# Attention masks added to the head biases on GpSimd instead of by products into the score banks, in a two-layer hybrid encoder

## The reference

```python
_, sel = lax.top_k(score, n_sel)                      # 64 admissible keys per query
logits = jnp.einsum('bqhd,bqkhd->bqkh', qb, k_sel) * ATTN_SCALE
logits = logits + bias_tab[t5_bucket(sel - qpos[None, :, None])]
logits = jnp.where(valid[..., None], logits, -1e30)
p = jax.nn.softmax(logits, axis=2)
return jnp.einsum('bqkh,bqkhd->bqhd', p, v_sel)
...
_, states = lax.associative_scan(combine, (a_seq, bu), axis=1)   # state-space branch
```

## Time and profile before

| what | us |
|---|---|
| median of 3 runs (1130.84 to 1132.05) | 1131.94 |
| the profiled execution | 1129.84 |
| its span | 1127.7 |
| PE busy in the span | 1115.2 (99%) |
| DVE, ACT, POOL busy | 756.5, 556.5, 405.6 |
| granted PE clock, mean | 0.998 |

### The profile page before, as it was taken

How to read it: one execution, slowest core, us unless ns; L and a number is a source line. 1 busy time by engine, 2 the same in 40 slices (tenths; PEclk the granted TensorE clock), 3 DMA queues, 4 the chain that set the end, 5 groups by cost and what they waited for, 6 DMA issues and landing times.

```text
span 1127.7 us, 17816 instructions
## 1 busy us (share of the span) xinstructions
PE 1115.2 (99%) x6020; PEld 922.6 (82%) x6020; DVE 756.5 (67%) x1082; ACT 556.5 (49%) x795; POOL 405.6 (36%) x567
## 2 busy tenths in 40 slices
PE   9999999999999999999999999999999999999997
PEld 7888778898788888888888888889877888888885
DVE  5656745789877865674586465468897787555544
ACT  6545433574673554454245444436747635454440
POOL 2889986107700478997700000011275000000001
PEclk9999999999999999999999999999999999999999
DMA  8866653645556586565367566536535566757541
GB/s 270 256 205 185 219 183 109 199 136 161 163 179 223 151 238 192 188 222 192 115 187 226 184 227 201 188 99 225 162 115 155 192 202 207 220 165 246 186 149 38
DMA packets 158720, 207.51 MB, mean 184 GB/s; under 512 B 13144, under 2 KB 107672, under 8 KB 158656
## 3 DMA queue, kind: packets, MB, share of 16 engines
q1 hardware_dynamic: 154928, 201.70, 55.9%
q10 hardware_dynamic: 2704, 3.36, 1.1%
q0 software_dynamic: 1024, 1.61, 0.8%
HBM read 205.56 MB, written 1.06 MB: 183 GB/s over the span
## 4 chain that ended last, share of the span: by engine, by line
PE 63%; POOL 18%; DVE 10%; issue 4%; DMA 2%; ACT 2%; SPq 1%; POOLq 0%; DVEq 0%; ACTq 0%
PE ps L719 19%; PE ps L721 18%; PE ps L720 18%; POOL small L1565 7%; DVE wlo L1215 5%; POOL b_bar L1565 3%; POOL tab_c L1565 2%; POOL tab_s L1701 2%; POOL tab_s L1565 1%; POOL tab_c L1698 1%; DVE score L1376 1%; DMA raw<-in_ffn_w_up 1%; PE ps L746 1%; PE ps L952 1%; DMA raw<-in_w_in 1%
## 5 line engine op out<-in xcount | busy, mean ns | idle before, releaser
L1215 DVE TENSOR_TENSOR wlo<-raw,whi 128x1024 fp32r<-128x1024 f32 (+1 forms) x372 | 479.7, 1306 | 197.1 <-ACT whi L411 183.4
L411 ACT CAST whi<-raw 128x1024 fp32r<-128x1024 f32 (+1 forms) x372 | 385.4, 1044 | 289.0 <-PE ps L721 221.1
L719 PE MATMUL ps<-whi,xh 128*128 128x512 f32 x990 | 390.7, 395 | 0.7 <-DVE wlo L1215 0.3
L721 PE MATMUL ps<-whi,xl 128*128 128x512 f32 x990 | 383.3, 387 | 0.0
L720 PE MATMUL ps<-wlo,xh 128*128 128x512 f32 x990 | 383.0, 387 | 0.0
L719 PEld LDWEIGHTS ps<-whi,xh 128*128 128x128 f32 x990 | 185.9, 188 | 43.3 <-issue 5.6
L721 PEld LDWEIGHTS ps<-whi,xl 128*128 128x128 f32 x990 | 185.9, 188 | 38.5
L720 PEld LDWEIGHTS ps<-wlo,xh 128*128 128x128 f32 x990 | 186.1, 188 | 35.3
L1589 POOL TENSOR_TENSOR rstd<-var_eps,cst 128x1 f32<-128x1 f32 x12 | 18.2, 1516 | 528.6 <-DVE var_eps L1262 528.6
L719 PE MATMUL ps<-whi,hh 128*128 128x512 f32 x352 | 139.6, 397 | 0.0
L721 PE MATMUL ps<-whi,hl 128*128 128x512 f32 x352 | 137.3, 390 | 0.0
(11 more groups left out here) (194 smaller groups left out, 1217.0 us busy)
## 6 DMA issues: line engine op xcount, KB each, us to landing
raw<-in_ffn_w_up SPq DMA_DIRECT2D x352, 256.0 KB, 4.0
raw<-in_ffn_w_down SPq DMA_DIRECT2D x176, 256.0 KB, 3.0
raw<-in_w_in SPq DMA_DIRECT2D x128, 256.0 KB, 3.3
raw<-in_w_branch SPq DMA_DIRECT2D x32, 256.0 KB, 3.3
raw<-in_w_out SPq DMA_DIRECT2D x32, 256.0 KB, 3.6
bias_g<-bias_rows ACTq DMA_DIRECT2D x16, 192.0 KB, 4.0
raw<-in_w_in SPq DMA_DIRECT2D x16, 148.0 KB, 2.2
affine<-in_ln_g SPq DMA_DIRECT2D x4, 512.0 KB, 5.3
```

Source lines behind the costliest of these rows:

```text
L411: nc.scalar.copy(whi[:, s % RING, 0:w], raw[:, s % RAW, 0:w]).then_inc(S["hi_done"], 1)
L719: nc.tensor.matmul(o, ah, bh, start=start, stop=False)
L721: return nc.tensor.matmul(o, al, bh, start=False, stop=stop)
L1215: nc.vector.tensor_tensor(wlo[:, s % RING, 0:w], raw[:, s % RAW, 0:w], f32(whi[:, s % RING, 0:w]), ALU.subtract).then_inc(S["split_done"], 1)
```

## The change

The two mask products, `ident_bf` and PE's wait for the mask go. POOL adds the mask to each head's bias window in SBUF (`add_bias`, two instructions a head, 16 a layer), and DVE's logits read the sum, `biased`, in place of `bias_g`. The windows get four buffers instead of two; ACT loads those of heads 0, 1 and of heads 4 to 7 (128 KB each instead of 192 KB), each pair of heads a pair of `exp_probs` earlier than before, and POOL's own queue loads those of heads 2 and 3 once the mask is done, as their buffer lies over the indexer's scores. In slots 7, 11 and 15 the scores now stand ahead of the turn.

```diff
     bias_g = place("bias_g", [P, 2, SEQ])
+    biased = place("biased", [P, 4, 3 * P])
...
+    bias_s = place("bias_s", [P, 2, SEQ])
...
             def load_bias(l, hd):
-                if hd >= 2:
-                    act.wait_ge(S["neg_max_ready"], N_HEADS * l + hd - 1)
+                if hd >= 4:
+                    act.wait_ge(S["bias_ready"], N_HEADS * l + hd - 3)
...
-                if p + 1 < N_PAIRS:
-                    load_bias(l, 2 * p + 2)
-                    load_bias(l, 2 * p + 3)
+                if p + 2 < N_PAIRS:
+                    load_bias(l, 2 * p + 4)
+                    load_bias(l, 2 * p + 5)
...
             def att_scores(l, p):
-                for e in range(2):
-                    nc.tensor.matmul(ps[:, score_bank(e), 0:3 * P], ident_bf[:, :], mask[:, :], start=True,
-                                     stop=False)
...
             def attention(l, j):
+                p, last = divmod(j - SCORES_AT, 4)
+                if last == 0 and 0 <= p < N_PAIRS:
+                    att_scores(l, p)
                 p, last = divmod(j - TRANSPOSE_AT, 4)
                 if last == 0 and 0 <= p < N_PAIRS:
                     prob_transpose(l, p)
-                p, last = divmod(j - SCORES_AT, 4)
-                if last == 0 and 0 <= p < N_PAIRS:
-                    att_scores(l, p)
...
             def att_logits(l, p):
-                    dve.wait_ge(g_landed[e], 16 * (N_PAIRS * l + p + 1))
+                    dve.wait_ge(S["bias_ready"], N_HEADS * l + 2 * p + e + 1)
...
-                            in1=bias_g[:, e, end - KEYS[i]:end][:, ::-1], scale=-1.0, scalar=3.0e38, op0=ALU.add,
+                            in1=biased[:, (2 * p + e) % 4, cols], scale=-1.0, scalar=3.0e38, op0=ALU.add,
...
+            def add_bias(l, p):
+                for hd in (2 * p, 2 * p + 1):
...
+                    if p >= 2:
+                        pool.wait_ge(S["neg_max_ready"], N_HEADS * l + hd - 3)
+                    for i in range(NT):
+                        cols = slice(i * P, i * P + KEYS[i])
+                        ins = nc.gpsimd.tensor_tensor(biased[:, hd % 4, cols], bias_of(hd)[:, 0:KEYS[i]][:, ::-1],
+                                                      mask[:, cols], ALU.add)
+                    ins.then_inc(S["bias_ready"], 1)
...
             def states(l):
-                for q in range(NQ):
-                    rotate_back(l, q)
-                    if q + 2 < NQ:
-                        make_decay(l, q + 2)
+                rotate_back(l, 0)
+                make_decay(l, 2)
+                rotate_back(l, 1)
+                pool.wait_ge(S["mask_ready"], NT * (l + 1))
+                pool.wait_ge(S["bias_stored"], 16)
+                for hd in (2, 3):
+                    pool.dma_start(bias_of(hd), bias_window(hd)).then_inc(early_landed[hd % 2], 16)
+                add_bias(l, 0)
+                add_bias(l, 1)
+                make_decay(l, 3)
+                rotate_back(l, 2)
+                add_bias(l, 2)
+                add_bias(l, 3)
+                rotate_back(l, 3)
```

More of the change, by code:

```diff
@@ L123, in build @@
     ident = sb("ident", [P, P])
-    ident_bf = sb("ident_bf", [P, P], BF16)
     parity = sb("parity", [P, P])
@@ L190, in build @@
     stg_at = at[0]
-    bias_g = place("bias_g", [P, 2, 3 * P])
+    bias_g = place("bias_g", [P, 2, SEQ])
+    biased = place("biased", [P, 4, 3 * P])
     at[0] = stg_at
@@ L195, in build @@
     stg = place("stg", [P, 2, NT, 512])
+    score_at = at[0]
+    bias_s = place("bias_s", [P, 2, SEQ])
+    at[0] = score_at
     score = place("score", [P, NT, SEQ])
@@ L215, in build @@
     x_landed = [sem(f"x_landed{i}") for i in range(3)]
-    g_landed = [sem(f"g_landed{i}") for i in range(2)]
+    g_landed = [sem(f"g_landed{i}") for i in range(4)]
+    early_landed = [sem(f"early_landed{i}") for i in range(2)]
     S = {}
@@ L223, in build @@
                  "proj_done proj_read pt_done pt_read bu_done bu_read decay_ready scan_done states_ready y_used "
-                 "idx_done relu_done weighted idx_added mask_ready s_done neg_max_ready exp_done prt_done prt_read "
+                 "idx_done relu_done weighted idx_added mask_ready bias_ready s_done neg_max_ready exp_done prt_done prt_read "
                  "pv_done inv_ready prob_ready yah_done ya_split bra_read y_sum gelu_done yh_done y_split gm_done "
@@ L304, in score_bank, with bias_of, bias_window @@
         return 4 if hd % 2 == 0 else 2
+    def bias_of(hd):
+        return (bias_g, bias_s)[hd // 2 % 2][:, hd % 2, :]
+    def bias_window(hd):
+        return bass.AP(bias_rows.tensor, hd * 512 + 1 + P, [[1, P], [1, SEQ]])
     def quarter(tab, q):
@@ L562, in load_bias @@
             def load_bias(l, hd):
-                src = bass.AP(bias_rows.tensor, hd * 512 + 1, [[1, P], [1, 3 * P]])
-                if hd >= 2:
-                    act.wait_ge(S["neg_max_ready"], N_HEADS * l + hd - 1)
+                if hd >= 4:
+                    act.wait_ge(S["bias_ready"], N_HEADS * l + hd - 3)
                 else:
@@ L569, in load_bias @@
                     act.wait_ge(S["bias_stored"], 16)
-                act.dma_start(bias_g[:, hd % 2, :], src).then_inc(g_landed[hd % 2], 16)
+                act.dma_start(bias_of(hd), bias_window(hd)).then_inc(g_landed[hd % 4], 16)
             def exp_probs(l, p):
@@ L993, in att_scores @@
                     pe.wait_ge(S["proj_read"], 2 * NPROJ * l + 8)
-                    pe.wait_ge(S["mask_ready"], NT * (l + 1))
                 else:
                     pe.wait_ge(S["neg_max_ready"], N_HEADS * l + 2 * p)
-                for e in range(2):
-                    nc.tensor.matmul(ps[:, score_bank(e), 0:3 * P], ident_bf[:, :], mask[:, :], start=True,
-                                     stop=False)
                 for i in range(NT):
@@ L1003, in att_scores @@
                         ins = nc.tensor.matmul(ps[:, score_bank(e), i * P:i * P + KEYS[i]], q_t[rows, p, tok(i)],
-                                               k_t[rows, p, 0:KEYS[i]], start=False, stop=i == NT - 1)
+                                               k_t[rows, p, 0:KEYS[i]], start=True, stop=True)
                 ins.then_inc(S["s_done"], 1)
@@ L1190, in _ @@
                 ffn(2 * l, 3 * l, first(l), 3 * l + 1, 0 if l == 0 else None)
-                if l == 0:
-                    pe.wait_ge(S["const_ready"], 2)
                 mixer(l)
@@ L1389, in att_logits @@
                         hold()
-                        end = (2 + i) * P
                         ins = nc.vector.tensor_tensor_reduce(
                             out=prob[:, e, cols], in0=ps[:, score_bank(e), cols],
-                            in1=bias_g[:, e, end - KEYS[i]:end][:, ::-1], scale=-1.0, scalar=3.0e38, op0=ALU.add,
+                            in1=biased[:, (2 * p + e) % 4, cols], scale=-1.0, scalar=3.0e38, op0=ALU.add,
                             op1=ALU.min, accum_out=neg_max[:, a:a + 1])
@@ L1534, in _ @@
             nc.vector.memset(k0_t[:, :, :], 0.0).then_inc(S["const_ready"], 1)
-            dve.wait_ge(S["ident_landed"], 16)
-            nc.vector.tensor_copy(ident_bf[:, :], ident[:, :]).then_inc(S["const_ready"], 1)
             x_lo(0, 0)
@@ L1540, in _ @@
             splits(2, 6)
-            dve.wait_ge(S["const_ready"], 2)
+            dve.wait_ge(S["const_ready"], 1)
             dve.wait_ge(S["const_landed"], 48)
@@ L1779, in rotate_back @@
                 op(h_im, h_im, h_tmp[:, :, :], ALU.add, S["states_ready"])
+            def add_bias(l, p):
+                for hd in (2 * p, 2 * p + 1):
+                    if p == 1:
+                        pool.wait_ge(early_landed[hd % 2], 16 * (l + 1))
+                    elif p == 3:
+                        pool.wait_ge(g_landed[hd % 4], 16 * (l + 1))
+                    else:
+                        pool.wait_ge(g_landed[hd % 4], 16 * (2 * l + p // 2 + 1))
+                    if p >= 2:
[5 more added lines that the diff above has]
+                    ins.then_inc(S["bias_ready"], 1)
             def states(l):
```

## The result

| what | before, us | changed, us |
|---|---|---|
| median | 1131.99 (1130.84 to 1133.65, 6 runs) | 1141.75 (1139.76 to 1144.86, 6 runs) |
| the profiled execution | 1129.84 | 1139.76 |
| its span | 1127.7 | 1137.7 |

The ratio is 1.0083 (95% interval 1.0065 to 1.010): slower by 9.8 us on the medians. 1143.5 was forecast. One execution of 1592.87 us, in the experiment with filler products, is in that kernel's median and in no ratio.

A forecast was written before the change was run, and what follows sets the result against it. PE's queue plus its few waits was taken to bound the kernel. Terms -3.4 + 3.3 + 1.0 + 11 = +11.9 gave 1141.7 for the profiled execution, 1143.8 on the median; forecast 1143.5 us, range 1130 to 1149.

The forecast's parts named there:

- term 4: At ssm_out(3), POOL's queue, lengthened by 16 additions a layer, ends late and PE stalls: 6 and about 5 us, +11.
- 1. mask products: In PE's queue, the mask products of eight pairs go, 0.42 us a pair, all on the path: -3.4 us.
- 2. pair 0 late: waits before the turns: Additions hold up DVE, pair 0's first logits come 2.4 us late, PE waits before both layers' turns: +3.3 us.
- 3. values behind the turn: With one slot between turn and values, PE waits for ACT's copy, mostly at pair 1: 0.5 a layer, +1.0 us.
- whatever leaves the queue is gained in full: Premise on PE's queue: time is its length plus few waits, so removed work counts fully; used for the masks' -3.4 us.
- each finds one gap: From 275 to 285 us, layer 0's eight additions each get between DVE's two-input instructions; DVE loses 3.6 us before deductions.
- POOL without idle time: Sign that the forecast is right: POOL shows no idle time from 275 to 320 us.
- the load of heads 2 and 3: Issued at 273.7 on POOL's queue, it was to land by 279, before addition 5, costing nothing.
- the scans run beside POOL: Rival: DVE's scans are not held up, term 2 about +1.5, term 4 about +4.5; total +3.6, 1135.5 us; chance 0.20.
- the additions fall into POOL's idle time: Rival: 9.1 us of additions a layer slip into POOL's 10.9 us idle, ssm_out(3) on time; 1128.4 us; chance 0.15.
- threshold of about 0.6 us an addition: Mean POOL time per addition under which the kernel was to be faster; at 1.0 and more the queue is late.
- The small sum: Rival: additions half held up, terms 2, 3, 4 at +1.5, +0.5, +2; total +0.6, 1132.5 us, no change; chance 0.15.

The follow-up runs named there:

- the experiment with filler products: Changed kernel with only the additions of pairs 0 and 1, plus nine useless products on PE ahead of pair 0's turn; 1136.57 us, ratio 1.0014.
- turns enforced: Changed kernel with a semaphore wait on POOL between any two additions (also called the links); 1145.81 us in one run, beside 1133.15 before.
- the additions of the first half alone: Changed kernel with only the additions of pairs 0 and 1, mask left out for heads 4 to 7; 1136.58 us, ratio 1.0048.
- the fills: Changed kernel with additions replaced by POOL fills that read nothing; 1131.17 us, ratio 0.9969; with each window fill done three times, 1128.24 us.

## Why the prediction was right, and where it was not

The direction, the total and the mechanism held: the additions exclude DVE's instructions with two inputs in SBUF, scans included, and PE waits at the turns and at `ssm_out(3)`. That the total came so near is in part luck: what the prediction did not have (waits before the scores and the clock, +4.8) made up for most of what term 4 had too much (7.2). Forecast against the trace, both layers:

| term | forecast | measured |
|---|---|---|
| 1. mask products | -3.4 | -3.4 (not measured by itself: eight times the 0.42 of the earlier trace rows) |
| 2. pair 0 late: waits before the turns | +3.3 | +3.6 (4.9 less 0.1 and 1.2) |
| waits before the scores of pair 1 | none | +1.5 |
| half clock behind these waits | none | +3.3 |
| 3. values behind the turn | +1.0 | 0 |
| 4. `ssm_out(3)` waits for POOL | +11 | +3.8 |
| small rest | | +0.6 |
| sum | +11.9 | +9.4 |

The clock's term is what is left of the cut to `ssm_out(2)`: 3.08 = 2.74 of added waits - 1.26 (three masks) + 1.6 in layer 0, and 1.6 again in layer 1. It agrees with the 1.7 us read from the windows of layer 0, and with the 3.1 us that the run with filler products gives for two layers.

1. **Mask products.** The size stands, but this term was not paid out in full: "whatever leaves the queue is gained in full" fails next to a wait. Without any addition the gain was 1.9 us of the 3.4 + 1.0 that the masks and the order could bring.
2. **DVE held up.** First logits 3.2 us late for 2.4 forecast. The wait before the turn of layer 0 is 2.13 for 2.0 only because PE had waited 0.72 before the scores just ahead, a place that the prediction did not have: together 2.85, the 0.8 us by which the logits were later still. In layer 1 it is 0.81 and 2.78, in sum 3.6 for 2.2 to 3.1. The step that failed inside is "each finds one gap": the first four additions ran back to back and one subtraction waited for all, 2.1 us for the 1.8 that four were to cost it (the 0.1 taken off a row's length has no row behind it). The first eight additions ended before the scans of quarter 2, so in layer 0 no scan took part in this delay. With turns enforced the delay was 2.6. The clock behind the wait, the largest part that the prediction left out, stood in no term.
3. **Values.** The changed kernel has no wait there. Without the additions it was 1.1 us, the size forecast, and mostly at pair 1, as forecast. With the additions of the first half alone it is gone, and with the clock kept full by the filler products 1.0 us is back: PE, held up by the clock, came later than the turned probabilities.
4. **POOL late.** This is the step that was mis-sized most, by 7 us, in three parts (layer 0, less 1.3): additions 1 to 8 ended at 282.8, not at 286.3, as four of them cost 2.08 us and not the contended price; POOL still waited 2.39 us for the scans ("POOL without idle time" was wrong) and 0.89 for the load of heads 2 and 3, which was to cost nothing, and `rotate_back(2)` started at 287.3, for 289.6. The last eight took 8.9 us for 7.8, `rotate_back(3)` 9.6 for 10.3, and the end came at 318.9 for 320.5. (The prediction's own steps add up to 321.0: 289.6 + 13.3 is 302.9, not 302.5, and the start that it calls 285 was 284.01 in its row.) The third part is PE: it arrived at 316.5 and not at 314.4, since the waits and the clock of term 2 had held it up longer. With 1.6 less on one side and 2.1 more on the other, the stall of 6 us became 2.4. Layer 1 was alike, 1.3 for 5.

The rivals: that the scans run beside POOL falls by the scans' own rows, longer beside the decay and, by 0.2 to 0.4 us, beside additions. The total alone would not have decided: 9.4 lies between that rival (+3.6) and the forecast (+11.9), and the rival's term 4 of +4.5 came nearer to the 3.8 measured than the forecast's +11. That the additions fall into POOL's idle time falls with their mean of 0.98 us; the fills show what that case looks like. Its threshold of about 0.6 us an addition is neither shown nor excluded. The small sum (+0.6) falls by the time.

## What to carry to other kernels

Before moving work to an engine that looks idle, ask whether its instructions share a read path with those of the engine that feeds the bottleneck: GpSimd with inputs in SBUF beside VectorE with two inputs in SBUF was paid on both queues in most of the additions here, and fills show how much of it is the sharing. Waits of the bottleneck engine in a row don't add up: a wait at one place makes it later at the next and shortens the wait there, and in the same way a saving ahead of a wait is partly waited out. Price a wait of TensorE of some 2 us with the clock it may cost behind it.

## What the runs showed of the hardware

- **Half clock after a short wait.** Waits of 2.13 (with 0.72 just ahead), 2.78, 2.91 and 3.39 us were followed by 1.2 GHz for some microseconds, about 1.6 to 3.4 us lost each. The waits of 2.88 us (at 142) and 2.43 us (at 320) in the changed kernel were not: the windows around them show 1.00. With the additions of pairs 2 and 3 alone the same wait at 142, 2.86 us, was followed by it (0.83 over 140 to 150), and with the links the wait of 2.15 before the first turn was not. So the wait's length alone does not tell.
- **Back-to-back instructions on POOL can keep DVE out.** Four additions of 0.4 to 0.7 us ran inside one subtraction (3.27 us), in both layers; with a semaphore between them they took 5.07 in turns with DVE. The next four took turns without one (5.10), so it is not a rule.
- **Scans are held up too**, up to 1946 ns for 1.2 us beside POOL's decay and 1.39 to 1.58 beside additions, though they are half as fast per column as a subtraction.
- **Fills on POOL don't touch DVE**: 11.1 us of them a layer moved the first logits by nothing.
